# First three latent tiles taken through each weight block together, scratch buffers of their own, and pairs of PSUM banks only at even numbers

## What is computed

```python
shift, scale, gate = adaln(c, w_mod, b_mod)                 # silu(c) @ w_mod + b, per sample
h = rms_norm(x, g_pre) * (1 + scale) + shift                # x: (16, 4096, 1024)
xa, ga, q, k, v, gb, gm = split_columns(h @ w_in)           # 512,512,1024,256,256,1024,2048
y_a = pool_mixer(xa, pool_w, pool_scale) * silu(ga)         # windows 2/4/8/16 minus the token
y_b = attend(rope(q), rope(k), v, k_ctx, v_ctx, sink) * silu(gb)   # keys within 128, and 256 context keys
g = sigmoid(gm)
merged = g[..., :1024] * (y_a @ w_branch_a) + g[..., 1024:] * (y_b @ w_branch_b)
out = x + gate * rms_norm(merged @ w_out, g_post)
```

## Time and profile before

| | us |
|---|---|
| median of 3 runs | 2393.46 |
| range of the runs | 2391.5 to 2394.12 |
| the profiled execution | 2388.5 |
| its span (slowest core, core 6) | 2387.0 |
| spans of the eight cores | 2370.8 to 2387.0 |

### The profile page before, as it was taken

One profiled execution on the slowest core, in us unless ns is written; L12 is line 12 of the kernel. 1 busy time (PEld: TensorE's weight loads), 2 busy tenths in 40 slices (PEclk: granted clock), 3 DMA queues, 4 the chain that ended last, 5 costly groups with the idle time before them and its releaser, 6 DMA issues.

```text
span 2387.0 us, 48262 instructions; the slowest of 8 cores (2370.8 to 2387.0 us)
## 1 busy us (share of the span) xinstructions
PE 2245.3 (94%) x17130; PEld 1114.9 (47%) x17130; DVE 945.0 (40%) x2316; ACT 1145.6 (48%) x1563; POOL 1005.7 (42%) x985
## 2 busy tenths in 40 slices
PE   5764999999999999999988999999999999999997
PEld 2332544554455445544543445544554455445543
DVE  1321344444444443444333444344434443444442
ACT  2221544554555455545544545554555455545553
POOL 1221444444444444444443444444444444444443
PEclk8897999999999999999999999999999999999999
DMA  9943333232323222222322232322232222232221
GB/s 248 210 69 58 73 64 68 59 70 63 70 64 69 63 67 68 69 63 63 72 72 76 69 67 60 73 67 67 60 75 66 66 60 70 69 68 59 69 53 47
DMA packets 320840, 176.86 MB, mean 74 GB/s; under 512 B 292064, under 2 KB 300384, under 8 KB 317792
## 3 DMA queue, kind: packets, MB, share of 16 engines
q1 hardware_dynamic: 318160, 156.83, 26.7%
q0 software_dynamic: 2448, 16.94, 4.5%
HBM read 87.93 MB, written 33.56 MB: 51 GB/s over the span
## 4 chain that ended last, share of the span: by engine, by line
PE 66%; DMA 12%; DVE 7%; POOL 5%; issue 4%; SPq 3%; ACT 2%; DVEq 0%; POOLq 0%; ACTq 0%
PE pball L481 33%; PE pball L691 8%; PE pball L563 6%; PE pball L612 5%; PE pball L587 5%; PE pball L672 4%; DMA s_hT<-s_xsb 4%; SPq L447 3%; DVE s_hT L471 3%; DMA s_mgT<-s_yb 3%; PE pball L662 2%; DMA s_kT<-s_krot 2%; ACT s_xsb L429 2%; POOL s_Gbr L597 1%; DMA gg_scr<-s_mu 1%
## 5 line engine op out<-in xcount | busy, mean ns | idle before, releaser
L481 PE MATMUL pball<-s_W,s_hT 128*128 128x512 bf16 x5152 | 1198.1, 382 | 17.8 <-DMA s_W<-w_all 5.5
L481 PEld LDWEIGHTS pball<-s_W,s_hT 128*128 128x128 bf16 x5152 | 485.8, 98 | 613.7 <-issue 74.2
L570 ACT ACTIVATE s_PT<-pball 128x1024 bf16<-128x1024 f32 x632 | 612.4, 1023 | 194.9 <-PE pball L563 194.9
L677 POOL TENSOR_TENSOR s_yb<-s_mu,s_mv 128x512 bf16<-128x512 f32 x126 | 159.6, 1267 | 516.2 <-DVE s_mv L674 498.9
L634 ACT ACTIVATE s_Tm<-pball 128x512 bf16<-128x512 f32 x256 | 152.8, 597 | 337.4 <-PE pball L481 331.7
L573 POOL TENSOR_SCALAR_AFFINE_SELECT s_PT<-s_PT 128x1024 bf16<-128x1024 bf16 x248 | 270.5, 1091 | 83.9 <-ACT s_PT L570 78.0
L691 PE MATMUL pball<-s_Wo,s_mgT 128*128 128x512 bf16 x1024 | 236.0, 381 | 15.8 <-DMA s_mgT<-s_yb 15.7
L672 PE MATMUL pball<-s_Wb,s_ybT 128*128 128x512 bf16 x1024 | 243.6, 381 | 2.2 <-DMA s_Wb<-w_all 1.3
L471 DVE TENSOR_SCALAR s_hT<-s_hT,s_gs,s_sh 128x128 bf16<-128x128 bf16 x536 | 126.8, 312 | 257.4 <-DMA s_hT<-s_xsb 257.2
L498 POOL TENSOR_TENSOR s_qrot<-s_rt 128x512 bf16<-128x512 f32 x128 | 162.3, 1268 | 94.6 <-DVE s_rt L494 78.4
L491 DVE TENSOR_TENSOR s_rt<-pball,s_ropet 128x512 f32<-128x512 f32 (+1 forms) x192 | 115.4, 601 | 196.6 <-POOL s_qrot L498 90.2
(11 more groups left out here) (98 smaller groups left out, 2076.2 us busy)
## 6 DMA issues: line engine op xcount, KB each, us to landing
s_xt<-x SPq DMA_DIRECT2D x64, 512.0 KB, 4.3
y<-s_xt SPq DMA_DIRECT2D x64, 512.0 KB, 2.7
s_W<-w_all POOLq DMA_DIRECT2D x10, 1024.0 KB, 25.5
s_Wb<-w_mod SPq DMA_DIRECT2D x2, 2048.0 KB, 16.8
s_Wo<-w_mod SPq DMA_DIRECT2D x2, 2048.0 KB, 24.4
s_ropet<-rope SPq DMA_DIRECT2D x64, 64.0 KB, 4.0
s_W<-w_mod SPq DMA_DIRECT2D x2, 2048.0 KB, 28.0
s_Wo<-w_all POOLq DMA_DIRECT2D x3, 1024.0 KB, 26.0
```

What stands on the lines that cost most here:

```text
L481: E("pe", lambda e, c=c: e.matmul(out=pb, lhsT=hT[h3][:, c, :], rhs=W[:, nb, c, :], start=(c == 0), stop=(c == 7)), reads=[bf(f"hT{h3}_{c} ...
L570: E("act", lambda e, s=s, j=j: e.activation(out=view(PT[s], 0, [[1, 1024]]), in_=pbv(j, 0, [[1, 1024]]), func=AF.Exp, scale=0.125), reads= ...
L677: E("pool", lambda e: e.tensor_tensor(out=mh_, in0=mu[:], in1=mv[:], op=ALU.add), reads=[bf("mu"), bf("mv")], writes=[bf(n) for n in mgn[rd]])
```

## The change

- `next_pair` takes pairs only at even banks.
- `attend` is split: `tile(k)` makes the steps of one tile (`qk`, `pv`, `gb`, `ga`, `gm`, `pool`, `A`, `B`, `mg`, `mgT`, `ybT`, `out`), so the steps of several tiles can be called in any order. `own` gives L0, L1 and L2 buffers of their own for q, gates, transposed results and so on. They lie in `Wo` (not loaded until late now), in the x buffers of slots 1 and 2, and in `PT` buffers. A fourth `hT` and a third rope buffer lie in `Wo` too, and a temporary buffer for L4's x. `inherit` carries old readers over to the new names.
- The opening is written out by hand to the end of L1's output. Each projection is done for L0, L1 and L2 before the next block is used. L3's k, v, q, xa are in it too, and L2's attention and gates. `attend` starts with L3, with L2 as its prior tile. All transposes up to there are on TensorE.
- Conditioning blocks 4 and 5 are loaded earlier, from GpSimd's queue, block 5 in the place of `W9/W10`. The gate store follows them, well ahead of the first `A`. Blocks 14 and 15 are loaded after the first `A` and `B`; the x tiles of L1, L2 and L4 are loaded again after their slots were used as scratch.
- `rope` in the opening alternates between two pairs of scratch buffers; the product behind the fold is made earlier.
- In the loop: x and rope of tile k+2 are issued at the head of `attend`; the sum of A and B (`mg`) is apart from `B`, and for half 0 comes after the next tile's k rotation; half 1 of A, B and its transposes come before the second group of key blocks.
- At the turn between samples the output projection comes after both q halves and its y store is put off into the next `attend`. The last tile of a sample does both `gb` and `ga` before the prior tile's output, and its `fin` uses `rt1`, `rt2`. At the very end the merged tile is transposed on TensorE.

```diff
         def next_pair():
-            j = min((q for q in range(NPB - 1) if not busy & {q, q + 1}), key=...)
+            j = min((q for q in range(0, NPB, 2) if not busy & {q, q + 1}), key=...)
...
+        Wof = flat(Wo, 8192)
+        xbf = [t[:].bitcast(BF16) for t in xs_]
+        hTs = [flat(t, 1024) for t in hT] + [Wof[:, 4096:5120]]
+        ropes = [flat(t, 128) for t in ropet] + [Wof[:, 7168:7424].bitcast(F32)]
+        xtmp = Wof[:, 0:4096].bitcast(F32)[:, 0:1024]
...
-        def load_wmod(blk):
-            t, o, bufs = wst[blk % 4]
+        def load_wmod(blk, eng="sp"):
+            t, o, bufs = wst[{4: 0, 5: 3}.get(blk, blk)]
...
-            qk((0, "self"), (0, "c0"))
-            if not early:
-                AB(0, False)
+            if k != L3 and prior:
+                issue_load(k + 2)
+            if turnover:
+                issue_load(k + 3)
+            t.qk((0, "self"), (0, "c0"))
+            AB(0)
             if nk is not None:
                 do_kv(nk)
-                if not early:
-                    do_kT(nk)
-            if prior and not early:
-                prior[3](0, *mg)
-            issue_load(k + 2)
-            if turnover:
-                issue_load(k + 3)
-            qk((0, "c1"), (0, "prev"))
-            if not early:
-                AB(1)
+                do_kT(nk)
+            if late_store:
+                late_store.pop()()
+            if prior:
+                prior.mg(0)
+                prior.mgT(0)
+            AB(1)
+            if prior:
+                prior.mg(1)
+                prior.mgT(1)
+            t.qk((0, "c1"), (0, "prev"))
...
+        alt = [(PTf[n], f"PT{n}") for n in (3, 4, 5)]
+        ctx_kv(C0, alt[0])
+        ctx_kv(C1, alt[1])
+        norm_T(L1)
+        norm_stat(L2)
+        ctx_kT(C0, alt[0])
+        do_kv(L0)
+        modulate(L1)
...
+        do_kv(L1, alt[2])
+        load_wmod(4, "pool")
+        load_wmod(5, "pool")
+        norm_T(L2)
+        do_q(L0, 0, 0)
...
+        do_q(L1, 0, 1)
+        do_qT(L0, 0, 0)
+        do_kv(L2)
...
+        do_xa(L2)
+        wload(7, W[:, 7], ["W7"])
+        t0.qk((1, "self"), (1, "c0"))
...
+        t0.gb(0)
+        norm_T(L3)
+        f = t0.pv(0)
+        t1.gb(0)
...
+        wload(8, W[:, 8], ["W8"])
+        t2.gb(0)
+        wmod_block(4)
+        t0.ybT(0)
+        t0.gb(1)
+        wload(11, Wa[:], ["Wa"])
...
+        t2.gb(1)
+        wmod_block(5)
+        wload(9, W[:, 9], ["W9"])
+        wload(10, W[:, 10], ["W10"])
+        wload(12, Wb[:, 0], ["Wb0"])
+        wload(13, Wb[:, 1], ["Wb1"])
+        store_gate()
+        load_gate(0)
...
+        load_x(L4, xtmp, [bf("xtmp")], "d_xtmp")
...
+        t0.gm(0, 1)
+        do_qT(L3, 1)
+        t1.gm(0, 1)
+        norm_stat(L4)
+        t0.gm(1, 1)
+        t1.gm(1, 1)
+        norm_scale(L4)
+        t0.A(0)
+        t0.B(0)
+        t0.mg(0)
+        wload(14, Wo[:, 0], [...])
+        wload(15, Wo[:, 1], [...])
+        norm_T(L4)
+        t1.A(0)
+        t1.B(0)
...
+        f0 = t0.out()
+        f0()
+        f1 = t1.out()
+        f1()
+        loaded.add(L4)
+        load_x(L4, xs_[0][:], [bf("xt0")], "d_x0")
+        late_out.append(t2)
+
+        for k in range(L3, NW):
+            if work[k][0] == "lat":
+                attend(k)
```

More of the change, by code:

```diff
@@ L233, in next_pair @@
         def next_pair():
-            j = min((q for q in range(NPB - 1) if not busy & {q, q + 1}), key=lambda q: max(pbuf[q].touch, pbuf[q + 1].touch))
+            j = min((q for q in range(0, NPB, 2) if not busy & {q, q + 1}), key=lambda q: max(pbuf[q].touch, pbuf[q + 1].touch))
             claim([j, j + 1])
@@ L527, in stage_ctx, with do_qT @@
[L527 to L532 removed]
+            rope(pb, pbb, 8, rslot(k), qrot, h * 512, bf(f"qrot{h}"))
+        def do_qT(k, nb, half=None):
+            h = nb if half is None else half
+            q_, qn = slots(k)["qT"]
+            turn(f"q{nb}", view(q_, nb * 512, [[128, 4], [1, 128]]), qrot[:, h * 512:(h + 1) * 512], [bf(f"qrot{h}")], [bf(qn[nb])])
@@ new lines, in ctx_kv, with ctx_kT @@
+        def ctx_kv(k, to):
+            pb, pbb = proj_tok(k, 0)
+            E("act", lambda e: e.activation(out=to[0][:, 0:256], in_=AP(pb.tensor, pb.offset, [pb.ap[0], [1, 256]]), func=AF.Copy), reads=[pbb], writes=[bf(to[1])])
+            v_copy(pb, pbb, vc[:, work[k][2], :, 0:64], bf("vc"))
+        def ctx_kT(k, to):
+            t = work[k][2]
+            turn("kc", kTc[:, :, t * 128:(t + 1) * 128], to[0][:, 0:256], [bf(to[1])], [bf("kTc")])
+        def stage_ctx(k):
+            ctx_kv(k, (krot, "krot"))
+            ctx_kT(k, (krot, "krot"))
@@ L670, in do_B @@
+            def do_B(rd):
                 pbk, pbkb = next_bank()
                 for c in range(8):
[L672 to L675 removed]
@@ L676, in do_B @@
-                mh_ = mg[:, rd * 512:(rd + 1) * 512]
-                E("pool", lambda e: e.tensor_tensor(out=mh_, in0=mu[:], in1=mv[:], op=ALU.add),
-                  reads=[bf("mu"), bf("mv")], writes=[bf(n) for n in mgn[rd]])
-            def do_mgT(rd, mg, mgn):
-                turn(f"m{rd}", mgT[:, rd * 4:rd * 4 + 4, :], mg[:, rd * 512:(rd + 1) * 512], [bf(n) for n in mgn[rd]], [bf(f"mgT{rd}")])
+                    E("pe", lambda e, c=c: e.matmul(out=pbk, lhsT=ybT_[:, c * 128:(c + 1) * 128], rhs=Wb[:, rd, c, :], start=(c == 0), stop=(c == 7)),
+                      reads=[bf(ybTn[c // 4]), bf(f"Wb{rd}")], writes=[pbkb], inc=(c == 7))
@@ new lines, in fin, with attend @@
+                    if now:
+                        store()
+                    return store
+                return fin
+            T_ = Steps()
+            T_.qk, T_.pv, T_.gb, T_.ga, T_.gm, T_.pool, T_.A, T_.B = qk, pv, do_gb, do_ga, do_gm, do_pool1, do_A, do_B
+            T_.mg, T_.mgT, T_.ybT, T_.out = do_mg, do_mgT, do_ybT, do_out
+            return T_
+        late_store = []
+        def attend(k):
+            _, b, i = work[k]
+            t = tile(k)
+            nk = k + 1 if i < NT - 1 else None
@@ L768, in attend @@
-            fin0 = pv(0)
-            qk((1, "prev"), (1, "c0"))
-            do_gb(1)
+                if fin is not None:
+                    fin()
+                if i == 0 and b > 0:
+                    load_gate(b)
+                fin0 = t.pv(0)
+                t.qk((1, "prev"), (1, "c0"))
+            else:
+                t.gb(0)
+                t.gb(1)
+                t.qk((0, "next"), (1, "self"))
+                t.ga()
+                fin = prior.out()
+                fin0 = t.pv(0)
+                t.qk((1, "prev"), (1, "c0"))
+                fin(True, ((rt1, "rt1"), (rt2, "rt2_0")))
@@ new lines, in build_program @@
+        fold()
+        inherit(["e_ga0", "e_ga1", "e_gb0", "e_gb1", "e_qb0", "e_qb1"], ["Wo0"])
+        inherit(["e_yT0", "e_yT1", "e_yT2", "e_yT3"], ["xt2"])
+        inherit(["e_pl0", "e_pl1", "e_tm1", "e_tm3"], ["xt1"])
+        t2 = tile(L2)
+        do_qT(L2, 0, 0)
+        norm_stat(L3)
+        do_q(L1, 1, 0)
+        do_qT(L0, 1, 1)
+        do_q(L2, 1, 1)
+        load_rope(L3)
+        load_rope(L4)
+        do_xa(L0)
+        do_qT(L1, 1, 0)
+        norm_scale(L3)
+        do_xa(L1)
@@ new lines, in build_program @@
+        t1.ybT(0)
+        t1.pool()
+        t1.qk((1, "prev"), (1, "next"))
+        t2.ga()
+        f = t1.pv(1)
+        do_kv(L3)
+        f()
+        do_xa(L3)
+        t1.ybT(1)
+        do_kT(L3)
+        t2.qk((0, "self"), (0, "c0"))
+        t2.qk((0, "c1"), (0, "prev"))
+        t0.gm(0, 0)
+        t2.qk((0, "next"))
+        t1.gm(0, 0)
+        f = t2.pv(0)
+        t2.qk((1, "self"))
+        t0.gm(1, 0)
+        f()
+        t2.qk((1, "c0"), (1, "c1"))
+        t1.gm(1, 0)
+        t2.ybT(0)
```

415 lines of the change are left out of this document (233 added, 182 removed).

## The result

The changed kernel takes 2297.3 us (median of 2296.58, 2297.27 and 2298.6) against 2393.1 us for the kernel before on the same chip: ratio 0.960, 95% interval 0.958 to 0.962, some 96 us less. The profiled execution took 2298.6 us with a span of 2297.0.

The account below looks back on a forecast made before the run. Idle TensorE time in the opening, up to about 228 us, was taken as the bound. Gains of 58.5 (opening), 0 (loop), 6 (turn) and 3 (end) took 2388.5 to 2321; plus 5.0 gave 2326 us, range 2303 to 2353.

Parts of the forecast that it names:

- Stage one: Opening from 53.5 us up to the first gate projection: 30.6 us of work, 39 at the old clock, plus 5 for chains.
- stage two: Opening from 98 us to L3's first key blocks: 90.9 us of work plus 2, 7 and 6 us, ending at 203.9.
- The wait for `Wo`: Before L0's output projection, for weight blocks 14 and 15: 4 to 16 us, taken as 6.
- Its 31 us lie beside matmuls then: Opening: the gate store, issued at about 130 us and landed at 162, is covered by matmuls before `mu` is written.
- Price 0 to 12 us; I take 0 beyond the 7: Opening: L4's x behind the gate load on SP, landing near 168 us, adds nothing beyond 7 us for chains and half clock.
- Rival (c): Opening: L4's x comes late behind the gate load on SP by its full 12 us, giving 2338 us; chance 0.08.
- Rival (a): Opening: first part wholly at half clock (+17), next 28 us at 0.78 (+8), giving 2351 us; chance 0.12.
- The merged half then comes up to 1.3 us later on GpSimd: Loop: later merge offset by transposes no longer behind two SP loads; priced at 0, bounds -5 to +12 us over 61 tiles.
- Even pairs: Loop: pairs only at even banks cost 0, since closest reuse, 2.6 us of matmuls, still exceeds two exponentials.
- Rival (e): Loop: even-bank pairs make each tile wait for a bank, 1.3 us a tile or 81 us, giving 2407 us; chance 0.03.
- The turn: Turn of the batch: output waits of 4.6 us and a k wait of 3.1 go, modulation costs 1.5 more; gain 6 us.
- The end: Kernel end: TensorE transposes replace DMA waits of 3.9 us, chains of 1.5 stay; with the split last tile, gain 3 us.

Follow-up runs that it names:

- x9: The kernel before with all four loop changes but its own opening, turn and end: 2365.94, 2368.77 and 2361.15 us, ratio to before 0.990.
- x5: The changed kernel with all four loop changes undone, its opening, turn and end kept: 2324.4 us, ratio to before 0.973.
- x3: The changed kernel with the merge of half 0 again ahead of the k rotation on GpSimd: 2323.7 us in one execution.
- x11: The kernel before with only its merge of half 0 put behind the k rotation on GpSimd: 2369.16 us, ratio to before 0.993.
- x1: The changed kernel with pairs of banks again allowed to start at an odd bank: 2297.07 us, ratio to before 0.961.
- x7: The changed kernel with store and load of the gate moved back to right before the first A: 2301.32 us, ratio to before 0.964.
- x6b: The kernel before with the gate vector in a buffer of its own instead of in `mu`: median 2371.6 us of six executions.

## Why the prediction was right and wrong

**The opening: right, with terms that offset each other.** Stage one was forecast for 98 us and ended at 97.5; L3 for 203.9 and came at 205.5 (203.1 in the mean of eight cores). Inside stage two two terms missed in opposite ways. The wait for `Wo`, taken at 6 us, was nothing: blocks 14 and 15 went out at 179.3 us, landed 10.7 and 16.2 us later (the two ends were taken from 18 and 30), and the output projection began at 198.5. "Its 31 us lie beside matmuls then" was right for `mu`, but the length was not: 32.5 us in the earlier trace rows became 44.5, beside four weight blocks as before, but issued closer ahead of it. The step "Price 0 to 12 us; I take 0 beyond the 7" is mis-sized: 5.2 us of wait and half-clock matmuls behind it. Rival (c) thus happened in part.

**The clock: better than forecast.** Rival (a), the half clock in stage one, did not come. The forecast itself took the old 0.78 for stage one; the stretch to 98 us was granted 0.96, the next 1.00. Stage one still ended at the forecast time, because two terms of it missed in opposite ways. TensorE's waits from 53.5 to 98 us in after:

```profile
PE pball L509 <- DVE s_hT L499: 3.7, 3, 2.2
PE pball L481 <- POOL s_qrot L535: 3.1, 3, 1.5
PE pball L622 <- DVE s_qT L483: 1.5, 1, 1.5
PE pball L509 <- DVE s_W L396: 1.0, 1, 1.0
PE pball L356 <- DVE s_mv L353: 1.0, 1, 1.0
```

The chains cost 10.3 us and not 5; the 30.6 us of work at a clock of 0.96 are 31.9 and not 39. The sum would be 42.2 us for the 44.0 measured. The 98 was right by some luck.

**The loop: the step that failed.** "The merged half then comes up to 1.3 us later on GpSimd, but its transposes are not behind two loads on SP. I price it at 0, bounds -5 to +12 over 61 tiles." The price was -22 to -27 us (x9 and x5), four to five times beyond the end at -5. The step followed the merged half, which the reordering makes later, and not the k rotation, which it makes earlier: by 0.55 us (it starts 3.17 us behind the k/v projection in after and 3.72 in before), since the merge of 1.26 us no longer stands ahead of it. The rotation was the one with a reader close behind: projection, VectorE's rope, rotation, transpose, scores, with the scores due just as the transpose landed. x3 (+26 us) and x11 (-19 us) show it from both sides. The view was also misread: "A steady tile takes some 34.1 us and leaves nothing to win" came from a stretch that was 33.9 of 34.0 busy, but matmuls overlap and their records stretch over short stalls (a matmul on `s_kT` lasts up to 632 ns in before, 377 in the median), so a busy share doesn't show losses of 0.2 to 0.4 us. 34.1 us was also at the good end of what before did (34.09 to 34.38 over its cores), and the slowest core sets the time.

**Even pairs: right.** Taken at 0, measured 0.2 us (x1), within the scatter. Rival (e) had no ground.

**The turn: about right.** The stretch gained 9.5 us instead of 6, but it holds ordinary tiles too. In x5, whose loop is the old one, it is 149.0 us where before has 155.8 (means of eight cores), a gain of 6.8; the rest is the loop's. **The end: wrong by nearly its whole 3 us.** It gained 0.2 on core 6 and 1.2 in the mean: the 3.9 us of DMA waits went, but TensorE waits 2.4 us for the last merge on GpSimd instead, and 1.6 us for exponentials in the split tile; the "chains of 1.5" were 4.0. (Of the forecast 3, 3.9 - 1.5 gives only 2.4; for the rest the prediction shows no row.) These rows of after are from 2200 us to its end:

```profile
PE pball L481 <- POOL s_yb L737: 2.4, 1, 2.4
PE pball L622 <- ACT s_PT L629: 1.1, 1, 1.1
PE pball L699 <- ACT s_PT L629: 0.5, 1, 0.5
```

**The last 5 us.** The forecast added 5.0 us because the profiled execution of before was that much under its median. In after the median is 1.3 us under the profiled one. That offset belonged to one execution and not to the kernel. So of the 29 us, 25 are the loop and 6 the offset; opening (-2.7), turn (+3.5) and end (-2.8) take 2 away. Core 6, on which the table above is made, is 0.9 us under the slowest core of after, which takes nearly 1 more, and the rest is rounding.

**The signs named ahead.** Right: no gap over 8 us after 53 us (the longest is 5.2, and 6.8 on core 4), L3 at 195 to 213 us, L666's wait gone, gate projections near 98. Wrong: the wait for `Wo` and the steady tile of 34.1 us, which is 33.8.

## What to carry to other kernels

When instructions on an in-order engine are swapped, follow the one that moves forward as well as the one that moves back, each to its reader, with the slack counted in tenths of a microsecond if it repeats in every tile. Whether a dense loop has slack is read from the distances between the starts of its steps over many tiles and all cores, against the same steps where nothing waits; the busy share doesn't show it, and the list of waits only in part. Compare all the cores of two kernels before you credit a change in one core's opening: the same code differed by 9 us there within one execution. The time of a tiny scattered DMA in a trace goes with its neighbours: moving it changes its length.

## What was not expected of the hardware

- A store of 2 x 4 KB in single elements took 32.5 us where four weight blocks had been issued 2 to 8 us ahead of it (before), 44.5 us where they were issued up to 2.5 us ahead (after), and 16.2 us with none (x7); over the cores 25 to 34, 35 to 49 and 11 to 21 us.
- Holding the gate vector apart (x6b) turned a 31.3 us wait into only 17 to 19 us of gain, since the weights behind it then came late.
- Stalls of 0.27 us in the mean tile, 16 us over 61 tiles, came with an order of two GpSimd instructions that was worth 19 to 26 us in all, while the listed waits on that transpose sum to 9.5 us.
